# In the first expert pair, the second half of the token gather stands behind the first weight's first half

## What is computed

```
def hier_moe(u, w_rg, b_rg, w_re, b_re, w1, w3, w2):
    x = u.reshape(-1, D_MODEL)                       # 264 x 1024
    ...                                              # a group of 4 experts, then 2 of its 4
    combine = jnp.einsum('tk,tke->te', wts, jax.nn.one_hot(eid, MOE_EXPERTS, dtype=F32))
    h = jax.nn.silu(jnp.einsum('td,edf->tef', x, w1)) * jnp.einsum('td,edf->tef', x, w3)
    y = jnp.einsum('tef,efd->td', h * combine[:, :, None].astype(h.dtype), w2)
```

## Time and profile before

| | |
|---|---|
| median of 3 runs | 1970.73 us (1969.31 to 1974.62) |
| span of the profiled execution | 1964.8 us; the median is 5.9 us more, which lies around the span |
| PE busy | 1897.6 us, 97% of the span |
| DVE, ACT, POOL busy | 811.9, 645.3, 119.4 us |
| HBM read | 600.39 MB of the span |
| mean granted PE clock | 0.983 of full speed |

### The profile page before, as it was taken

The page is one execution under the profiler, slowest core; times in us unless marked ns, Lnnn a source line. Parts: engine busy times, 40 slices in busy tenths (PEclk is TensorE's granted clock), DMA queues, the critical chain, the costliest instruction groups (busy, mean ns, idle before and its releaser), DMA issues. The chain is left out here.

```text
span 1964.8 us, 28506 instructions
## 1 busy us (share of the span) xinstructions
PE 1897.6 (97%) x11091; PEld 1188.8 (61%) x11091; DVE 811.9 (41%) x1908; ACT 645.3 (33%) x1508; POOL 119.4 (6%) x100
## 2 busy tenths in 40 slices
PE   9999999999999887899999999999999999999999
PEld 7877764444777564644445887644437877764443
DVE  4699242232203359242332363323315699242232
ACT  3489121212112217222122425221213489122111
POOL 0233000000100000000000000000000233000000
PEclk9999999999999879999999999999999999999999
DMA  9888949999837986579999468599997788959997
GB/s 333 258 298 257 368 193 420 421 421 403 284 98 264 302 278 292 216 324 421 420 421 340 138 225 329 228 422 420 421 410 238 243 295 265 369 197 421 421 420 327
DMA packets 243172, 629.74 MB, mean 321 GB/s; under 512 B 14184, under 2 KB 169112, under 8 KB 193352
## 3 DMA queue, kind: packets, MB, share of 16 engines
q1 hardware_dynamic: 231176, 613.88, 82.9%
q0 software_dynamic: 2368, 8.48, 1.4%
q10 hardware_dynamic: 9472, 5.28, 0.9%
HBM read 600.39 MB, written 35.56 MB: 324 GB/s over the span
## 5 line engine op out<-in xcount | busy, mean ns | idle before, releaser
L753 PE MATMUL bank<-uT,ring 128*128 128x264 f32 x1280 | 301.1, 394 | 2.4 <-DVE s_xbc L1088 2.4
L1767 PE MATMUL bank<-late,e_room 128*64 128x512 f32 x1280 | 281.1, 593 | 0.6 <-DMA late<-in_moe_w 0.6
L753 PEld LDWEIGHTS bank<-uT,ring 128*128 128x128 f32 x1280 | 245.2, 194 | 51.2 <-issue 7.0
L1767 PEld LDWEIGHTS bank<-late,e_room 128*64 128x64 f32 x1280 | 90.6, 137 | 180.9 <-issue 178.6
L1608 DVE TENSOR_TENSOR e_room<-e_room,bank 128x512 f32<-128x512 f32 x32 | 22.0, 688 | 367.5 <-PE bank L1767 367.5
L1767 PE MATMUL bank<-ring,e_room 128*64 128x512 f32 x768 | 169.7, 594 | 0.0
L1813 PE MATMUL bank<-late,e_room 128*64 128x512 f32 x640 | 143.1, 595 | 6.5 <-DMA late<-in_moe_w 3.8
L1614 DVE TENSOR_TENSOR xT<-xT,bank 128x512 f32<-128x512 f32 x112 | 69.5, 682 | 142.3 <-PE bank L1841 142.3
L1944 ACT ACTIVATE e_room<-bank 128x512 f32<-128x512 f32 x32 | 19.1, 598 | 319.5 <-PE bank L1767 319.4
L850 PE MATMUL bank<-s_xbc,ring 128*128 128x264 f32 x512 | 116.4, 388 | 3.8 <-ACT s_xbc L995 3.8
L1767 PEld LDWEIGHTS bank<-ring,e_room 128*64 128x64 f32 x768 | 53.7, 137 | 106.0 <-issue 105.5
(11 more groups left out here) (548 smaller groups left out, 2477.5 us busy)
## 6 DMA issues: line engine op xcount, KB each, us to landing
late<-in_moe_w SPq DMA_DIRECT2D x240, 1024.0 KB, 19.1
ring<-in_moe_w SPq DMA_DIRECT2D x144, 1024.0 KB, 15.7
ring<-in_m_w_in SPq DMA_DIRECT2D x40, 1024.0 KB, 9.1
late<-in_ssm SPq DMA_DIRECT2D x32, 512.0 KB, 6.7
out_ssm_s<-late SPq DMA_DIRECT2D x32, 512.0 KB, 4.0
ring<-in_m_w_out SPq DMA_DIRECT2D x16, 1024.0 KB, 9.3
late<-in_cache_cmp SPq DMA_DIRECT2D x64, 256.0 KB, 4.8
ring<-in_h_w_in SPq DMA_DIRECT2D x16, 1024.0 KB, 5.8
```

The lines of the kernel that those rows point to most:

```text
L753: mm = nc.tensor.matmul(bank[p % 3][:, 0:T], W.view(s, KT, 256)[:, k, c:c + 128], uT[:, k], start=(k == 0), stop=(k == KT - 1))
L1767: mm = nc.tensor.matmul(bank[b][CAP * j:CAP * j + CAP, :], xg[:, EK // 2 * h + k, CAP * j:CAP * j + CAP], rows_of(p, key)[:, k], start=(h ...
```

## The change

PE no longer gathers the second half of the sample rows in front of the branch: `gather_decode(1)` stands in `gathered_program`, behind `gather_first(0)`. `gather_first(1)` stands in pair 0, behind the first half of w1. DVE copies the sample rows of the second half at once, but fills the second half of `xg` behind `combine`, no longer in front of it. The counter of the sample gathers becomes two, one for each half, and the dense program raises the second one in its place.

```
-                    for h in range(2):
-                        dve.wait_ge(*dec_gathered.at(1 + h))
+                        dve.wait_ge(*dec_gathered[h].at(1))
...
-                        dve.wait_ge(*dec_kept.at(1 + h))
-                        dve.wait_ge(*gathered.at(1 + h))
-                        fill_first(h)
+                        if h == 0:
+                            dve.wait_ge(*dec_kept.at(1))
+                            dve.wait_ge(*gathered.at(1))
+                            fill_first(0)
                     combine(comb_done)
+                    dve.wait_ge(*dec_kept.at(2))
+                    dve.wait_ge(*gathered.at(2))
+                    fill_first(1)
                     free_places(comb_done)
...
                             if h == 1:
                                 mm.then_inc(*(gate_filled if b == GATE else up_filled).one())
+                            elif p == 0 and b == GATE:
+                                gather_first(1)
...
                     gather_first(0)
-                    gather_first(1)
+                    gather_decode(1)
...
-                for h in range(2):
-                    gather_decode(h)
+                gather_decode(0)
```

More of the change, by code:

```diff
@@ L1383, in moe @@
         dec_made, dec_added = count("dec_made"), count("dec_added")
-        dec_gathered, dec_kept, xg_copied = count("dec_gathered"), count("dec_kept"), count("xg_copied")
+        dec_gathered = [count("dec_gathered"), count("dec_gathered_far")]
+        dec_kept, xg_copied = count("dec_kept"), count("xg_copied")
         comb_made = count("comb_made")
@@ L1393, in moe @@
                           from_row_ready: PAIRS, hg_ready: PAIRS, xg_ready: 2 * PAIRS, x_added: 4 + 4 * (PAIRS - 1) + KT, w_row_ready: 1,
-                          to_row_ready: 1 + 3 * (PAIRS - 1), comb_done: 6 + 16 + 5, dec_kept: 2, xg_copied: 2 + 4 * (PAIRS - 1)}
+                          to_row_ready: 1 + 3 * (PAIRS - 1), comb_done: 6 + 16 + 5, dec_kept: 2, dec_gathered[1]: 1, xg_copied: 2 + 4 * (PAIRS - 1)}
         if layer < 3:
@@ L1752, in gather_decode @@
                                               start=True, stop=True)
-                    mm.then_inc(*dec_gathered.one())
+                    mm.then_inc(*dec_gathered[h].one())
                 def pair(p, last):
@@ L1908, in dense_program @@
                         sum_x(pe, norms[1], 1)
-                    leave(pe, gathered_total, (gate_filled, up_filled, turned, down_filled, gathered, back_filled, weights_turned, dec_made))
+                    leave(pe, gathered_total, (gate_filled, up_filled, turned, down_filled, gathered, back_filled, weights_turned, dec_made, dec_gathered[1]))
                 pe.wait_ge(*first_rows.at(1))
                 pe.wait_ge(*act_done.at(3))
-                for h in range(2):
-                    gather_decode(h)
+                gather_decode(0)
                 pe.wait_ge(*first_rows.at(2))
```

## The result

The changed kernel takes 1984.68 us (median of 7 runs), the kernel before, beside it on the same chip, 1973.54: a ratio of 1.0044 [1.0028, 1.0060], or +8.7 us [5.5, 11.8]. Forecast was 1971.5 us, no change, in a range of 1968.0 to 1976.0. The profiled execution has a span of 1981.0 us.

The account below looks back on a forecast made before the run. In the expert stage, weight DMA and PE end within about 1 us of each other. Layer ends of +0.34, -0.06, +0.06 and +0.42 sum to +0.76, say +0.8, on 1970.73: 1971.5 us, range 1968.0 to 1976.0.

Parts of the forecast that it names:

- G unmoved: At the branch: the first gather starts no earlier, since loading flag and branch set it; PE idles there about 1.1 us.
- G: The start of the first gather on PE behind the branch, at 1742.53 in layer 3 of the kernel before.
- A colder instruction stream behind the branch: Behind the branch: example given for the unseen causes, which together had chance 0.05; no size of its own.
- clock rival: Layer head: idle gaps let PE's clock fall, 1.7 us lost per layer, +7.6 in all, 1978.3 us; chance 0.05.
- w1 starts at G + 3.17: Layer head: the first w1 matmul waits 0.35 us for `xg` and comes 3.17 us behind the first gather, before 3.76.
- the 0.59 us earlier: Weight stream at the layer head: SP issues the first two transfers 0.59 us earlier, with the earlier first w1 matmul.
- one weight and half: Layer head on PE: span from w1's start, 3.44 us; with the second gather's 1.88, w3 starts at G + 8.49.
- waits for weights in the last pair: Expert stage's end: PE's later arrival uses up these waits, leaving them nearly gone, 0 to 0.2 us.
- brackets: PE's idle times for weights in the last pair before the change: 0.95, 1.35, 1.23 and 0.87 us, layers 0 to 3.
- The rival that the gathers ahead of the branch hold G: At the branch: four fewer matmuls let the first gather come earlier, about -1.4 us in sum, 1969.3 us; chance 0.15.
- hole in the stream: DMA between the first transfer pairs: 1.47 us lost instead of 0.5, +3.5 in all, 1974.2 us; chance 0.10.
- no earlier start: Layer head: the first w1 matmul stays at G + 3.76, PE 1.88 us late, +3.1, 1973.8 us; chance 0.05.

Follow-up runs that it names:

- e1: Changed kernel with four more matmuls at the end of layer 0's dense program, not executed, which shift the code behind them: 1.005.
- e3: Kernel before with only the sample gather's second half moved behind the branch; the token gather's second half stays ahead of the first weight: 1.0078.
- e9: Changed kernel with one filler matmul of 128x8 behind the first sample gather, ahead of the branch: 1.0010.
- e10: Changed kernel with the first transpose repeated twice more right behind the branch hint, nothing added at the branch: 1.0052.
- e16: Changed kernel with one filler transpose (2 instructions) behind the first sample gather, ahead of the branch: 0.9997.
- e17: Changed kernel with an added PE wait for ACT's fourth copy in layers 0 and 3, on the second of three earlier router matmuls: 1.0040.
- e13: Changed kernel with an added PE wait for ACT's fourth copy in layers 0 and 3, ahead of the last pair of router matmuls: 1.0029.
- e18: The change with one of the second sample gather's four matmuls left ahead of the branch, the other three behind the first token gather: 1.0009.
- e8: Changed kernel with PE's wait for the second signal on the first rows moved ahead of the first sample gather: 1.0041.
- e2: Kernel before with 60 more matmuls at the end of layer 0's dense program, not executed, which shift the code behind them: 0.9994.
- e11: Kernel before with the branch hint moved behind 8 of the 16 transposes that follow it: 1.0002.
- e12: Kernel before with the branch hint moved behind all 16 transposes that follow it: 1.0000.
- e15: Changed kernel with the branch hint behind the first router matmul that waits for DVE: 1.0074, from three timed runs.
- e14: Kernel before with the branch hint behind the first router matmul that waits for DVE: 0.9997.
- e4: Kernel before with only the token gather's second half moved behind w1's first half; both sample gathers stay ahead of the branch: 0.9996.

## Why the prediction was wrong, point by point

**"G unmoved" is the step that failed.** G was to follow the flag by 1.33 to 1.54 us as before. In layers 1 and 2 it does: 846.10 is 1.34 us behind layer 1's flag, layer 2 has 1.35. In layers 0 and 3 the branch, which was taken as a fixed price, waits for code: +2.95 and +3.16 us. I had read the gap before DVE's first operation and PE's idle time as the price of a branch, but not asked what keeps that price low. The branch rows of before (362 to 597 ns) and the two code transfers ahead of each could have told that something is hidden there, and the spacing of such transfers (3.2 to 3.7 us) was an estimate of what losing it costs. "A colder instruction stream behind the branch" was named among the unseen, with no price and a chance of 0.05.

**The clock rival held in part.** It asked whether a gap of about 1 us lets the clock fall. In layer 2 of the changed kernel 0.87 us did, and cost 1.53 us up to w1 (forecast for the rival: 1.7). In layer 1 0.85 us did not. Over the kernels with a gap of 0.72 to 0.87 us in layer 2 the clock fell in seven of eight (after, e1, e3, e9, e10, e16, e17, not e13), in layer 1 with 0.71 to 0.86 in none. With 0.62 (e18) it fell in neither, and in layer 0 not with 0.93 and 0.95 (e9, e16). In e8 PE idles for 0.81 us ahead of the sample gather in both layers, and the clock fell in layer 1 (0.51 from 847 to 850 us) and not in layer 2. Behind the gaps of 4 us it fell every time. So this rival was underweighted at 0.05, but it would have moved layer 2 alone, as in e9 and e16.

**What held.** e18 is the change with that step repaired. Its G is 1.53, 1.33, 1.33 and 1.40 us behind the flag. w1 starts at G + 3.17 in all four layers (273.80 - 270.62 = 3.18 from the rounded rows), as forecast. SP's first transfer of layer 3 goes out at G + 6.85, which is the 0.59 us earlier that was forecast against G + 7.44 in the earlier trace rows. w3 starts at G + 8.74 in place of 8.49, so one weight and half with the gather behind it was sized 0.25 us too small, and all of PE behind it is 1.54 us late, not 1.29. The stage ends:

```
             layer 0   layer 1   layer 2   layer 3   sum
forecast       +0.34     -0.06     +0.06     +0.42   +0.76
e18            +0.34     -0.07     +0.08     +0.18   +0.53
after          +4.64     -0.10     +1.56     +5.66  +11.76
```

The waits for weights in the last pair are gone in both kernels, and nothing was gained by it: PE came 1.54 us later, where the sum said 1.29. That e18 comes within 0.23 us of the forecast's sum is luck in part. The delay was sized 0.25 us too small in each layer; the waits that it uses up had cost 1.18, 1.57, 1.45 and 1.30 us and not the 0.95, 1.35, 1.23 and 0.87 of the brackets. The two errors cancel. The rival that the gathers ahead of the branch hold G is settled too: with 16, 18, 20 or 32 instructions there, G follows the flag by 1.22 to 1.58 us whenever the fetch is kept. The rivals of the hole in the stream and of no earlier start did not come true: no DMA wait is left in the last pair.

**What stays open.** Why 16 instructions lose the fetch and 18 keep it, and why layers 1 and 2, which run the same code from the hint on, keep it with 16. The runs exclude the place of the target (e1 and e2 in layer 0, e9 against e10 in layer 3), the distance from the hint (e10, e11, e12), a need for 1 us of array time (e9, e16) and, in layer 3, the time at which the sequencer passes the wait (e13, e17). e15 suggests a race between the hint and the sequencer's way to the branch, since two layers with the same times part there; it was seen once and not tested further.

## What to carry to other kernels

Before instructions are taken away from the front of a branch, read the branch's own row and the code transfers ahead of it: a branch of 0.4 us whose code was fetched in advance can become one of 3.5 us, and the views call that wait "issue". Where a change saves little, its cheap parts decide: here a single matmul left in place (e18, 1.0009 for 1.0044) is worth some 7 of the 8.7 us. Look at every layer for itself; a repeated stage can lose a fetch or its clock in one layer and not in the next.

## What the runs showed of the hardware that was not expected

- A hinted branch whose code transfer has not started lasts 3.0 to 3.9 us in 15 of 17 cases, against 0.36 to 0.61 with it; in the other two, layer 0 of e13 and e17, the transfer started 0.1 us ahead of the branch, which lasted 2.42 and 2.21 us.
- The jump at the start of PE's part of layer 0 waits for code too, in some kernels: 2.75 to 3.11 us in e9, e13, e14 and e17, with a code transfer that starts 0.4 to 0.7 us behind its begin, against 0.41 us in the others.
- Where the fetch is kept, the second code transfer starts 3.0 to 3.8 us behind the first (not counting e14 and e15, whose hint comes later), though one moves its 16 KB in 0.9 to 1.4 us.
- Instructions whose result nobody uses can protect such a fetch: 2 more ahead of the branch (e16), with a matmul row of 0.27 us, took 3 us away.
- PE idle for 1.11 us right behind the first gather (e4) left the clock at 1.00 in all layers; behind an idle time of 0.87 us right ahead of it, it fell in layer 2. The first gather of 16 rows lasts 2.05 us at 2.4 GHz and 3.78 at 1.2.
